# Exchanging the rotary halves by transfers inside SBUF instead of permutation products, in three attention layers of an eight-layer transformer kernel

## The reference, cut to what matters

```python
def rope(x, pos):
    half = HEAD_DIM // 2
    inv = jnp.float32(ROPE_THETA) ** (-jnp.arange(half, dtype=jnp.float32) / half)
    ang = pos.astype(jnp.float32)[:, None] * inv[None, :]
    cos = jnp.cos(ang)[None, :, None, :]
    sin = jnp.sin(ang)[None, :, None, :]
    xf = x.astype(jnp.float32)
    x1, x2 = xf[..., :half], xf[..., half:]
    return jnp.concatenate([x1 * cos - x2 * sin, x2 * cos + x1 * sin], axis=-1).astype(x.dtype)
```

## Time and profile before

| | |
|---|---|
| median of 3 runs | 2395.06 us (2391.28 to 2395.19) |
| span of the profiled execution, first to last instruction | 2389.1 us |
| TensorE busy | 2321.5 us, 97% |
| VectorE busy | 1288.7 us, 54% |
| ScalarE busy | 955.4 us, 40% |
| GpSimd busy | 446.0 us, 19% |
| moved by the DMA engines | 203.80 MB, mean 85 GB/s |
| mean granted clock of TensorE | 0.993 |

### The profile page before, as it was taken

One profiled execution on the slowest core, in us unless ns is written; L12 is line 12 of the kernel. 1 busy time (PEld: TensorE's weight loads), 2 busy tenths in 40 slices (PEclk: granted clock), 3 DMA queues, 4 the chain that ended last, 5 costly groups with the idle time before them and its releaser, 6 DMA issues.

```text
span 2389.1 us, 30420 instructions
## 1 busy us (share of the span) xinstructions
PE 2321.5 (97%) x11616; PEld 1836.2 (77%) x11616; DVE 1288.7 (54%) x1690; ACT 955.4 (40%) x1401; POOL 446.0 (19%) x431
## 2 busy tenths in 40 slices
PE   9999999999999989999999999999999999999998
PEld 7775668888888658888887668888888757888887
DVE  6447646664546666665456864333346585433333
ACT  4328853443323473343334353322324763322222
POOL 0003434110005125110004034200122004211010
PEclk9999999999999999999999999999999999999999
DMA  5221002222233112322223212222222202222222
GB/s 187 106 71 36 2 4 89 102 91 102 88 105 108 42 37 88 106 88 95 98 89 131 71 54 88 105 89 106 93 101 100 86 5 84 88 106 88 106 101 76
DMA packets 31494, 203.80 MB, mean 85 GB/s; under 512 B 4260, under 2 KB 5288, under 8 KB 7720
## 3 DMA queue, kind: packets, MB, share of 16 engines
q1 hardware_dynamic: 30104, 199.37, 23.5%
q10 hardware_dynamic: 1296, 3.15, 0.4%
HBM read 200.41 MB, written 2.10 MB: 85 GB/s over the span
## 4 chain that ended last, share of the span: by engine, by line
PE 86%; DVE 6%; ACT 5%; issue 2%; POOL 1%; DMA 0%; SPq 0%; POOLq 0%; ACTq 0%; DVEq 0%
PE D L585 74%; PE X L696 3%; PE D L710 3%; PE D L718 2%; ACT prob L1331 1%; DVE w_lo L1671 1%; ACT w_hi L1124 1%; ACT prob_t L1124 1%; PE X L702 1%; DVE prob L2007 1%; PE X L821 1%; PE X L651 0%; DMA w_raw<-in_weights 0%; DVE xg L1699 0%; DVE conv_out L1825 0%
## 5 line engine op out<-in xcount | busy, mean ns | idle before, releaser
L585 PE MATMUL D<-xg,w_hi 128*128 128x512 f32 x3184 | 988.5, 392 | 4.6 <-DVE w_lo L1671 2.7
L585 PE MATMUL D<-mid,w_hi 128*128 128x512 f32 x2308 | 713.7, 390 | 16.7 <-DVE mid L1671 6.9
L585 PEld LDWEIGHTS D<-xg,w_hi 128*128 128x128 f32 x3184 | 597.8, 188 | 133.3 <-issue 5.8
L585 PE MATMUL D<-xg,w_lo 128*128 128x512 f32 x1592 | 620.6, 390 | 0.0
L1671 DVE TENSOR_TENSOR w_lo<-w_raw,w_hi 128x2048 fp32r<-128x2048 f32 (+2 forms) x210 | 459.7, 2190 | 288.5 <-ACT w_hi L1124 288.4
L1124 ACT ACTIVATE w_hi<-w_raw 128x2048 fp32r<-128x2048 f32 (+2 forms) x210 | 355.9, 1695 | 594.1 <-PE D L585 590.3
L585 PEld LDWEIGHTS D<-mid,w_hi 128*128 128x128 f32 x2308 | 433.1, 188 | 111.0 <-issue 12.0
L585 PE MATMUL D<-mid,w_lo 128*128 128x512 f32 x1154 | 449.7, 390 | 0.0
L585 PEld LDWEIGHTS D<-xg,w_lo 128*128 128x128 f32 x1592 | 299.6, 188 | 62.9
L1733 DVE TENSOR_TENSOR h<-D,h 128x1024 f32 (+1 forms) x71 | 86.9, 1224 | 352.8 <-PE D L585 352.7
L585 PEld LDWEIGHTS D<-mid,w_lo 128*128 128x128 f32 x1154 | 216.9, 188 | 45.5
(11 more groups left out here) (284 smaller groups left out, 1811.0 us busy)
## 6 DMA issues: line engine op xcount, KB each, us to landing
w_raw<-in_weights SPq DMA_DIRECT2D x184, 1024.0 KB, 4.8
h<-in_x SPq DMA_DIRECT2D x4, 512.0 KB, 7.5
out_y<-h SPq DMA_DIRECT2D x4, 512.0 KB, 2.9
w_raw<-in_weights SPq DMA_DIRECT2D x2, 512.0 KB, 6.8
inv_cnt<-in_inv_cnt ACTq DMA_DIRECT2D x1, 1024.0 KB, 4.8
cos<-in_cos ACTq DMA_DIRECT2D x3, 256.0 KB, 4.8
sin<-in_sin ACTq DMA_DIRECT2D x3, 256.0 KB, 5.2
vec<-in_vec SPq DMA_DIRECT2D x1, 272.0 KB, 2.8
```

The costliest lines, as they stand in the source:

```text
L585: last = nc.tensor.matmul(out, w[a], x[b], start=start and k == 0, stop=stop and k == 2)
```

## The change

The halves are exchanged by four transfers inside SBUF for every copy, issued by ScalarE behind that copy; ScalarE first waits for the copy's own semaphore. The minus sign goes into the table `sin`. The permutation products and their places in TensorE's program go, with the waits that they needed; `X` is no longer read by the rotary. The compressed keys of `nsa` and the layer `odd` keep their permutation products.

```diff
+            def swap_halves(out, x, done):
+
+                for r in range(0, P, HD):
+                    upper, lower = slice(r, r + HD // 2), slice(r + HD // 2, r + HD)
+                    act.dma_start(out[upper], x[lower]).then_inc(done, 16)
+                    act.dma_start(out[lower], x[upper]).then_inc(done, 16)
+
             def queries_out(l, u, n):
...
                 copy(zq[:, :, :], D[:, 2 * s:2 * s + 2, :]).then_inc(d_free[s], 1)
+                act.wait_ge(d_free[s], u // 2 + 1)
+                swap_halves(rope_t, zq, q_rot)
 
             def key_value(u):
...
                 copy(vz2[:, :], D[:, 2 * s + 1, :]).then_inc(d_free[s], 1)
+                act.wait_ge(d_free[s], u // 2 + 1)
+                swap_halves(kzr, kz2, k_rot[0])
...
                     copy(kz[:, n], D[:, 2 * s:2 * s + 2, :]).then_inc(d_free[s], 1)
+                    act.wait_ge(d_free[s], (u + n) // 2 + 1)
+                    swap_halves(ktr[:, n], kz[:, n], k_rot[n])
                     split_high(w1 + n)
```

```diff
-            def swap(u, out):
-
-                pe.wait_ge(d_free[u % 2], u // 2 + 1)
-                for j in range(2):
-                    last = nc.tensor.matmul(out[:, j, :], perm[:, :], zq[:, j, :], start=True, stop=True)
-                last.then_inc(q_rot, 1)
...
-                project(q + 1, x_norm, middle=query_swap(q, 0))
-                project(q + 2, x_norm, middle=query_swap(q + 1, 1))
+                project(q + 1, x_norm)
+                project(q + 2, x_norm)
                 pe.wait_ge(kv_low, 4)
-                project(at["kv"], x_kv, middle=query_swap(q + 2, 0))
-                pe.wait_ge(q_ready, qpairs_before[l] + 2)
-                project(at["q_last"], x_norm, middle=lambda: key_swap(at["kv"], 1))
+                project(at["kv"], x_kv)
+                project(at["q_last"], x_norm, middle=lambda: turn_values(at["kv"], 3))
...
-                link(nc.vector.scalar_tensor_tensor(rope_t[:, :, :], X[:, 2 * pair:2 * pair + 2, :], scale,
+                link(nc.vector.scalar_tensor_tensor(rope_t[:, :, :], rope_t[:, :, :], scale,
                                                     sin[:, :].unsqueeze(1).to_broadcast(two), ALU.mult, ALU.mult))
...
+                if sign and fn is np.sin and r % dim < half:
+                    t[first_row + r] *= -1.0
```

More of the change, by code:

```diff
@@ L795, in attend @@
                             pe.wait_ge(evac, a0 + n)
-                        elif kind == "nsa":
-                            for v in range(u, u + 2):
+                        elif kind != "odd":
+                            for v in (u, u + 1) if kind == "nsa" else (u - 1, u):
                                 pe.wait_ge(d_free[v % 2], v // 2 + 1)
-                        elif kind in SINK0:
-                            pe.wait_ge(q_half, late_before[l] + 1)
                         turn(kind, units[n], a0 + n)
@@ L839, in out_product, with turn_values @@
                         project(at["out"] + j, x_mid(0), i=i)
-            def key_swap(u, pair):
+            def turn_values(u, bank):
                 pe.wait_ge(d_free[u % 2], u // 2 + 1)
-                nc.tensor.matmul(X[:, 2 * pair, :], perm[:, :], kz2[:, :], start=True, stop=True).then_inc(k_rot, 1)
                 for t in range(QT):
-                    last = nc.tensor.transpose(X[:, 2 * pair + 1, span(t)], vz2[:, span(t)], ident[:, :])
+                    last = nc.tensor.transpose(X[:, bank, span(t)], vz2[:, span(t)], ident[:, :])
                 last.then_inc(v_turned, 1)
@@ L894, in compressed_hidden @@
                     last.then_inc(w_used, 1)
-                    if z == 0:
+                    if z == 0 and middle is not None:
                         middle()
@@ L2126, in nsa @@
                     split_low(w1 + n)
-                    dve.wait_ge(k_rot, krope_before[l] + n + 1)
+                    dve.wait_ge(k_rot[n], SWAP)
                     two = [P, 2, SEQ]
-                    nc.vector.tensor_tensor(kt[:, 0], kz[:, n], cos[:, :].unsqueeze(1).to_broadcast(two), ALU.mult)
-                    link(nc.vector.tensor_tensor(kt[:, 1], X[:, 2 * n:2 * n + 2, :],
-                                                 sin[:, :].unsqueeze(1).to_broadcast(two), ALU.mult))
+                    nc.vector.tensor_tensor(kt[:, :], kz[:, n], cos[:, :].unsqueeze(1).to_broadcast(two), ALU.mult)
+                    link(nc.vector.tensor_tensor(ktr[:, n], ktr[:, n], sin[:, :].unsqueeze(1).to_broadcast(two),
+                                                 ALU.mult))
                     for half in range(2):
                         for side in range(2):
-                            ins = nc.vector.tensor_tensor(kdup[rows_of(side), half::2, n, :], kt[rows_of(half), 0],
-                                                          kt[rows_of(half), 1], ALU.add)
+                            ins = nc.vector.tensor_tensor(kdup[rows_of(side), half::2, n, :], kt[rows_of(half)],
+                                                          ktr[rows_of(half), n], ALU.add)
                     ins.then_inc(k_ready, 1)
@@ L2160, in nsa @@
                 split_low(at["v"] + 1)
-                query_rotary("nsa", l, 3, 0)
+                query_rotary("nsa", l, 3)
                 compressed_max(0)
@@ L2183, in swa @@
                         key_value_low(2 * n + 1)
-                key_rotary(l, 2)
-                attend("swa", l, at["out"], 3, at["q_last"])
+                key_rotary(l)
+                attend("swa", l, at["out"], 3)
                 last_phase(l)
@@ L2238, in even @@
                     scale_block(l)
-                query_rotary("even", l, 0, 0)
-                attend("even", l, at["out"], 1, at["q_last"])
+                query_rotary("even", l, 0)
+                attend("even", l, at["out"], 1)
                 last_phase(l)
@@ L2667, in constants @@
     tokens = np.arange(SEQ)
-    c["cos"], c["sin"] = table(HD, tokens, P, 0)
+    c["cos"], c["sin"] = table(HD, tokens, P, 0, sign=True)
     c["cos_m"], c["sin_m"] = table(MLA_ROPE, tokens, P, 0)
```

85 lines of the change are left out of this document (33 added, 52 removed).

## The result

The change made the kernel slower: 2401.26 us (median of 8 runs, 2397.59 to 2405.73) against 2392.94 us for the kernel before (8 runs, 2391.28 to 2396.96). The ratio is 1.0036, with a 95% interval of 1.0026 to 1.0045: 8.3 us more where the prediction said 3.0 more. It lies inside the range of 2388 to 2405, and beyond the 0.2% that counts as no change.

The account below looks back on a forecast made before the run. TensorE, busy 97% of 2389.1 us, was taken to bound the kernel. nsa -5.9, swa +4.5 and even +4.4 summed to +3.0 us, on a median of 2395.1 giving 2398.1 us, range 2388 to 2405.

Parts of the forecast that it names:

- the term d: Behind each of 14 copies, ScalarE's four issues make everything later in its program 2.0 us late; bounds 1.4 to 2.6.
- nsa: nsa layer: removed exchanges gain, partly lost in waits before the second keys and q_last; -5.9 us.
- swa, up to kv: swa before unit kv: kv starts 3.1 us later, TensorE idles 7.9 us, and slow clock behind it costs 2.2.
- even: Layer even: q_last's wait grows from 2.52 to 4.5 us, attention starts 1.6 later, plus late pair and clock; +4.4 us.
- The late pairs: Last query pair of swa and even: VectorE waits for the landing, 1.8 us each; even's clock fall half counted, 1.0.
- (3): Late waits in swa and even: landing takes 5 us, not 2.5; +8.0, 2403.1 us; chance 0.22.
- (1): All copies: issuing does not hold ScalarE up, lateness 0.2 us; together -14.8, 2380.3 us; chance 0.07.
- (2): Prices at lower ends: lateness 1.5, landing 2.0, no clock fall in even; -4.1, 2391.0 us; chance of gain over 0.2% 0.13.

Follow-up runs that it names:

- nsa alone: Kernel before with transfers in the nsa layer only (six of fourteen exchanges), issued by ScalarE; 2389.52 us, ratio 0.9978 to the kernel before.
- The kernel with the products put back: Changed kernel with unneeded products on TensorE in the places of nine removed pairs (six nsa, three swa); 2407.88 us, ratio 1.0057 to the kernel before.
- the one with late products: Changed kernel with the last query pair of swa and of even exchanged by permutation products again; 2395.43 us, ratio 1.0005 to the kernel before.
- the GpSimd kernel: Changed kernel with the same four transfers per copy issued by GpSimd instead of ScalarE; 2386.26 us, ratio 0.9966 to the kernel before.
- nsa alone by GpSimd: Kernel before with transfers in the nsa layer only, issued by GpSimd; 2383.62 us, ratio 0.9957 to the kernel before.
- the kernel with eight: Changed kernel with each exchange in eight transfers of half the columns instead of four; 2427.10 us, ratio 1.0143 to the kernel before.

## Why the prediction was off, point by point

The mechanism and the places were those of the prediction; the sum was 5 us short. **The step that was off is the term d**, the lateness of what stands behind a copy, with four issues at 0.39 + 3 x 0.45, gaps and 0.2 for the wait: 2.0 us. Measured: issues of 0.51 + 3 x 0.61 with gaps, and with the overlap of two instructions that is lost, 2.7 in all, above the upper bound of 2.6. The 0.2 for the wait, for which no row was given, is borne out: the issue starts 0.04 us behind the copy's end, the next instruction 0.10 behind the last issue, and before it began 0.10 ahead of the copy's end. The issues themselves were dearer than those of the table loads: 0.51 us for the first of four, where the first table took 0.35 to 0.39. A single transfer of 128 rows inside SBUF took 0.47, so the cut into 32 rows is a small part of it; what makes the rest is not shown.

- *nsa.* The keys' wait grew from 5.22 to 6.55 us (7.7 said), but TensorE resumed only 0.4 us earlier (75.16 against 75.58, 0.9 said). The difference is slow clock, which the prediction did not have between the two halves of the wait: from 66 to 70 us it is 0.59, where it was 1.00. So of the 3.44 us taken away 0.4 came through, 1.3 are in the waits and an estimate of 1.6 (0.41 of 4 us) in the slow clock. q_last waits 2.56 us for its weights (1.9 said, 2.6 with the measured d). With d at 2.7 the predicted -5.9 becomes -4.5; nsa alone measured -4.6.
- *swa, up to kv.* The chain passes ScalarE's issues twice, behind the first copy and behind the second, so the wait of 7.9 us becomes 9.3: measured 8.99. From the first copy to kv it is 26.1 us before and 30.6 now, 4.4 more (3.1 said, 4.5 with the measured d). The slow clock behind it came as said, 0.50 for the 4.4 us of the window.
- *even.* q_last: 4.5 us said, 5.2 with the measured d. The kernel with the products put back shows 5.25, this profile 6.55, the one with late products 5.94. In the last two ScalarE's four issues there took longer. In this profile single ones took up to three times as long as usual:

```profile
1349.16 1.01 ACTq L1313 DMA_DIRECT2D rope_t<-zq  x1
1350.21 1.55 ACTq L1312 DMA_DIRECT2D rope_t<-zq  x1
...
1352.50 1.91 ACT L1085 ACTIVATE w_hi<-w_raw 128x2048 fp32r<-128x2048 f32 x1 [3.92 <-issue]
```

- *The late pairs.* The landing took 2.3 us, not 2.5, and VectorE began 4.2 us behind the copy's end, against 4.0 said:

```profile
816.10 1.02 ACT L1085 ACTIVATE zq<-D 128x1024 f32<-128x1024 f32 x1 [4.35 <-PE D L586]
...
819.70 0.40 ACT L1292 ACTIVATE prob<-prob,neg_max 128x129 f32<-128x129 f32 x1 [2.57 <-issue]
...
821.32 1.22 DVE L2015 SCALAR_TENSOR_TENSOR rope_t<-rope_t,sin 128x1024 f32<-128x1024 f32 x1 [3.34 <-DMA rope_t<-zq]
```

What was too small is the price of this wait. In swa the low clock from 820 to 824 costs nothing, since TensorE was busy for 0.20 us of it. But it stays at 0.50 up to 832, while in the kernel before it had come back in part by then:

```profile
828.00:832.00 4.00, 4.00 (x28) 2.49 (x28) 2.89 (x14) 2.84 (x9) 1.59 (x6) 0.64 0.01 2
```

In even it fell for 1380 to 1384, which had been counted half. By the runs the two pairs cost 8.3 - 1.5 = 6.8 us, where 1.8 + 1.8 + 1.0 = 4.6 had been put down. The fall of the earlier trace rows in swa is not a fixed part of the kernel before either: the two kernels with transfers in nsa alone have the same program there, and their clock is 1.00 for the whole stage, which is 1.3 us shorter. The prediction took one execution's clock for the kernel's.

With d at 2.7 and the late waits 0.2 longer the prediction's own sum is -4.5 + (4.5 + 1.4 + 0.2) + (4.4 + 0.7 + 0.2) = +6.9 us. The 1.4 us that are missing to 8.3 are of the size of the further falls of the clock; they were not taken apart from the rest by an experiment. That the result lies inside the range is in part luck: d lay outside its own bounds, and the upper end of the range was set for a slow landing, which did not come.

**The rivals.** (3), a slow landing, was not the cause although the time came out near it: no landing of these transfers took more than 3.8 us, and the median was 2.3. (1), that issuing doesn't hold ScalarE, is false for ScalarE, and the GpSimd kernel is the case it described: -14.8 had been worked out for it, -7.7 was measured. Its nsa term was right (-9.8 against -10.5 for nsa alone by GpSimd). The late pairs were not: they wait as long as in the changed kernel or longer, 5.45 and 4.88 us. Nor was kv, where TensorE still waits 3.99 us. (2), the prices at their lower ends, is on the wrong side: d was 2.7, not 1.5.

**The Trainium skill.** The issue took 0.51 to 0.61 us of ScalarE here, and the changed kernel's loss hangs on it. The Trainium skill, DMA: Bandwidth & Descriptors, Anatomy of one DMA, gives its some 50 ns of dispatch and its total, 2.0 us and the bytes over 436 GB/s, for transfers that GpSimd issues; the prediction set them beside ScalarE's, for which that section has no figure. Where the section applies, in the GpSimd kernel, an issue took 0.49 us of GpSimd, of which the page's dispatch can be only a small part, and the landing of 128 KB took 2.7 us, where an estimate by the page's total is 2.3. That ScalarE's landings took 2.3 agrees with this estimate, but is not what the page speaks of.

## What to carry to other kernels

Before work is moved from a busy TensorE to transfers, price the issues on the engine that begins them, and look at what is next in its program: here a microsecond more behind each of fourteen copies, 14 us of ScalarE in all, came back as some 5 to 10 us of the kernel, although ScalarE is busy for 40% of the span only. Let an engine issue whose program is empty there (16 us of difference for the same transfers), and leave the product where its result is waited for at once. And ask of each removed product who ends the next wait: nine pairs of 15.5 us on TensorE were worth 5.6 in the changed kernel. A profile shows one execution's clock; before a wait's slow clock is put into a sum, see whether it comes in another execution too.

## What the runs showed of the hardware

- One issue of a transfer inside SBUF by ScalarE takes 0.51 us as the first and 0.61 behind another (32 rows), 0.47 with 128 rows; by GpSimd 0.49. Half the bytes in each (64 KB) make it no cheaper: 0.61 in the kernel with eight.
- The landing takes 2.3 us for 128 KB from ScalarE, 2.0 for 64 KB and 2.9 for one transfer of 512 KB of 128 rows; 2.7 from GpSimd. Cutting a tile into four makes each landing shorter and the last one begin three issues later; what it costs is the issuer's time.
- Single issues of ScalarE took up to 1.55 us, of GpSimd 0.72 at most in its three kernels. What the long ones met is not known.
- Behind one and the same wait the clock may fall or not. Behind 2.56 to 2.57 us before q_last of nsa the first record took 1.22 us in the changed kernel, 1.09 with transfers in nsa alone and 0.73 with the late pairs by products, all three with the same program up to there. Behind 2.52 us in even it took 0.74 us in the kernel before and 1.12 with GpSimd's issues; behind 2.74 us in the odd layer 0.73 before and 1.22 in the changed kernel. With GpSimd's issues the 4 us behind the wait in even ran at 0.57, an estimate of 1.7 us lost.
- The executions of one kernel differ by their clock. The eight of the changed kernel have spans of 2395.8 to 2403.9 us at mean granted clocks of 0.987 down to 0.984. The changed kernel has more long waits and its runs spread over 8.1 us, against 5.7; that the one is the cause of the other was not tried.
